# Layer norms of a three-block transformer kernel: residual added ahead, down tiles in turn, gain inside the product, high part direct, low parts awaited apart

## The chip, the cores and the metric

One core of one Trainium2 chip runs the whole program. The metric is device time in microseconds for one execution, start to end. Five engines matter: TensorE (PE, matmul; PEld is its weight load), VectorE (DVE), ScalarE (ACT), GpSimd (POOL) and SyncE (SP), which here issues all the loads. Each engine runs its own instruction stream in order and waits on semaphores.

## The reference

The reference is a stack of three blocks on x of 512 positions by 1024 features, in float32.

```
block 1 (fox):   h = forgetting-gate attention(x);  x = LN(a*x + h); f = conv_ffn(x); x = LN(a*x + f)
block 2 (diff):  h = differential attention(x);     x = LN(a*x + h); f = conv_ffn(x); x = LN(a*x + f)
block 3 (ssd):   h = attention branch + state space branch of rms_norm(x)
                 x = x + rms_norm(h);  x = x + rms_norm(swiglu_ffn(rms_norm(x)))
LN(y) = (y - mean(y)) * rsqrt(var(y) + 1e-5) * g + b       a = 4 ** 0.25, mean over the 1024 features
rms_norm(y) = y * rsqrt(mean(y*y) + 1e-6) * g
```

## The kernel before

**Layout.** Activations are feature major: 8 blocks of 128 features (partitions) by 512 positions. A block `j` of the tensor `XH` is `blk(XH, j)`. Every linear product keeps float32 accuracy by splitting each operand in two parts, a high part rounded to the matmul's type (`XH`, `HI`) and a low part, the rest (`XL`, `LO`). A product of one 128x128 weight block with one 128x512 block of x is three matmuls: HI with XH, HI with XL, LO with XH.

**Order of the work.** A planner, `agenda()`, writes one list of steps; the five engine programs walk it and each picks out its own part of each step. Weights come in units of up to 8 k-blocks by 256 columns. `take` starts a unit, and during its matmul steps (`step_of`, each followed by `tick`) the parts of the next unit are split: ACT writes HI (L1530), DVE (L1899) or POOL (L2382) writes LO. The units named `bqk`, `bv`, `aqk`, `av` have all their LO parts made by POOL, the others alternate. `tick` also advances a side stream (`beside`, the attention of the block). PSUM banks go round in `lin["banks"]`; in the first units of block 3 only banks 0 and 1 are in the ring. `XH` and `YH` are the same memory, and so are `XL` and `YL`.

**The norms.** There are eight, named a0, f0, a1, f1 (layer norms after attention and feed-forward of blocks 1 and 2), c0, m, p, f (RMS norms of block 3). For each tile of the last product before a layer norm, `residual` does, on DVE, two steps `YL = a*XL + PS` (L1928) and `YH = a*XH + YL` (L1932), and `accumulate` puts an `acc` step: ACT squares YH (L1548), POOL adds the square to `A2` (L2402) and, for layer norms, YH to `A1` (L2404). Tiles 0 to 6 are added so; tile 7's YH and its square go to the sums directly. `statistics` is then the following chain:

- `stat0`: PE adds the columns of A2, of A1, of YH block 7 and of the last square with matmuls of one column (`mm(PS[6]...MEAN[:, 0:1])`, 8 records for each). ACT meanwhile loads the table of the square root (L1551).
- `stat1`: DVE copies both sums (L1937), squares the mean (L1939), subtracts (L1942); PE spreads the mean over PS5 (8 records). `stat2`: ACT takes the root (L1557), DVE the reciprocal (L1945). `stat3`: PE spreads it over PS6 (8 records).
- `ln` for each of 8 blocks: DVE subtracts (L1953, `t = PS5 - YH`), DVE multiplies (L1956, `t = t*PS6`), ACT applies gain and bias (L1566, the gain negated). `lnx`: ACT copies t to XH (L1570), POOL writes XL = t - XH (L2382). For f1 the result goes to XR instead and feeds the sums of c0.

The first unit after a norm (`up0`, `up1`, `up2`, `bqk` 0, `ck` 0) is walked k-block by k-block (`together=True`), each matmul step waiting for XL of its k-block. The RMS norms c0 and p make their blocks with one DVE product (L1963), ACT's copy (L1574) and POOL's low part. For m and f, ACT first copies the tile out of PSUM (`cye`, L1578) and squares the copy.

A down projection (`ffn_down`, `lin_long`) makes two tiles at once over 22 k-blocks in three units, matmul step by matmul step in alternation, so that both tiles end together.

Of the kernel before, what the change touches and what calls it, by code (L numbers as in the profile page):

```python
# [110 lines left out]
def const_arrays():  # L111
# [52 lines left out]
    "stat0": (("ssum", 1),),  # L164
    "stat1": (("smu", 1), ("svar", 1)),
    "stat2": (("ssd", 1), ("srs", 1)),
    "stat3": (("spr", 1),),
    "ln": (("lt", 1), ("la", 1)),
# [65 lines left out]
class Agenda:  # L234


    def __init__(self):
        self.steps, self.tiles, self.order, self.bank_of, self.free_of = [], [], [], {}, {}
        self.unit_end, self.count = {}, {}
# [15 lines left out]
def raised(step, tiles):  # L255
# [3 lines left out]
    if k in ("mm", "mt"):  # L259
        return (("lin", 1),) if step[2] in tiles[step[1]].incs else ()  # L260
# [8 lines left out]
    if k == "acc":  # L269
        _, n, j, mean = step  # L270
        adds = (1 if j == 0 else 2 if j < 7 else 0) if mean else (1 if 0 < j < 7 else 0)
        return (("sq", 1),) + ((("ac", adds),) if adds else ())
# [23 lines left out]
def unit_sequence():  # L296
# [9 lines left out]
    out += [("ck", 0), ("cq", 0), ("cq", 1), ("cv", 0)] + [("cx", i) for i in range(6)] + [("cz", i) for i in range(4)]  # L306
# [7 lines left out]
def agenda():  # L314
# [116 lines left out]

    def lin_fm(key, src, widths=(128, 128), together=False, before=None, evac=None):
# [3 lines left out]
        for j, w in enumerate(widths):  # L436
            tiles.append(Tile(made, sum(widths[:j]), w, banks[j], src))
        pairs = [(j, kk) for kk in range(len(made)) for j in range(len(widths))] if together else \
                [(j, kk) for j in range(len(widths)) for kk in range(len(made))]
        for j, kk in pairs:  # L440
            if before is not None:
                before(kk)
            step_of("mm", t0 + j, kk)
            tick()
            if evac is not None and kk == len(made) - 1:
# [14 lines left out]
    def lin_long(keys, src):  # L460
        banks = [pick(), pick()]
        t0 = len(tiles)
# [3 lines left out]
        kk = 0  # L466
        for key in keys:
            take(key)
            for k in range(places[key][1]):
                for j in range(2):  # L470
                    step_of("mm", t0 + j, kk)
                    tick()
                kk += 1
        return [t0, t0 + 1]
# [17 lines left out]
    def statistics(n, mean):  # L492
        at_bank(put("stat0", n, mean), 6)
        if mean:
            at_bank(put("stat1", n), 5)
# [3 lines left out]
        if mean:  # L499
            freed[5] = ("spr", ("stat3", n, mean))  # L500

    def layer_norm(n, final=None):
        statistics(n, True)
        for j in range(8):
            s = put("ln", n, j)
            freed[5] = freed[6] = ("lt", s)
            if final is None:
                x_step[j] = put("lnx", n, j)
            else:
                accumulate(final, j, False)  # L510

# [129 lines left out]
    def ffn_down(lay, evac):  # L641
        for i in range(4):
            for j, t in enumerate(lin_long([("dn" + lay, i, p) for p in range(3)], "H" + lay)):
                evac(2 * i + j, t)
# [1943 lines left out]
```

## Time and profile before

| what | value |
|---|---|
| median of 3 runs | 2434.15 us (2431.7 to 2441.45) |
| profiled execution, its own time | 2443.44 us |
| its span, first to last instruction | 2441.6 us |
| PE busy | 2254.6 us, 92% |
| DVE, ACT, POOL busy | 1096.0, 1001.4, 974.8 us (45%, 41%, 40%) |
| granted TensorE clock, mean | 0.946 of 2.4 GHz |

The page gives one profiled execution. A clock of 1.00 in a stretch is 2.4 GHz, 0.50 is 1.2 GHz. In a timeline row the first number is the start, the second the duration, and the bracket says how long the engine sat idle before it and which engine's instruction ended the wait. Float32 matmuls of the sums show as two records for each instruction.

### The profile page before, as it was taken

How to read it: one execution, taken by the hardware profiler on the slowest of the kernel's cores; microseconds unless marked ns; L12 is line 12 of the kernel's file. 1: busy time of each engine (PE TensorE's matmuls, PEld its weight loads, DVE VectorE, ACT ScalarE, POOL GpSimd, SP SyncE). 2: the span in 40 equal slices, each digit the busy share in tenths (PEclk: the TensorE clock that was granted, in tenths of full speed). 3: DMA queues.
4: the chain of work that ended last, by engine and by line, in shares of the span. 5: the costliest groups of instructions: out<-in, count | busy, mean ns of one | idle time of the engine just before them, and what ended most of it. 6: DMA issues, size and time to landing. Idle time of an engine off the chain costs nothing.

```text
span 2441.6 us, 28073 instructions
## 1 busy us (share of the span) xinstructions
PE 2254.6 (92%) x10880; PEld 1841.6 (75%) x10880; DVE 1096.0 (45%) x1774; ACT 1001.4 (41%) x2015; POOL 974.8 (40%) x760
## 2 busy tenths in 40 slices
PE   7999999999979887999999789996899997999997
PEld 6778778888867776788888666664687885888886
DVE  3545555553345764555443333546545234232222
ACT  5665454443254553444442244443344234232222
POOL 3554644333455641644334351103423345232232
PEclk9999999999989998999999887997999997999998
DMA  4111222222212220222322111110012221222221
GB/s 152 51 65 58 70 87 91 100 101 95 97 61 75 77 83 18 70 101 90 104 97 95 59 46 35 35 35 18 18 44 95 86 104 52 104 87 104 97 95 50
DMA packets 29844, 183.07 MB, mean 75 GB/s; under 512 B 3984, under 2 KB 4112, under 8 KB 11920
## 3 DMA queue, kind: packets, MB, share of 16 engines
q1 hardware_dynamic: 29712, 181.27, 21.5%
q8 instruction: 87, 1.43, 0.2%
q14 instruction: 45, 0.37, 0.0%
HBM read 174.97 MB, written 2.10 MB: 73 GB/s over the span
## 4 chain that ended last, share of the span: by engine, by line
PE 84%; DVE 5%; ACT 4%; POOL 4%; issue 2%; DMA 1%; SPq 0%; POOLq 0%; ACTq 0%; DVEq 0%
PE PS L1239 82%; PE PS L1332 1%; POOL LO L2382 1%; POOL XL L2382 1%; PE PS L1442 1%; DVE bQS L1899 1%; DVE cCVT L2266 0%; DVE aQS L1899 0%; DMA RAW<-wall 0%; POOL A_p L2402 0%; POOL bROT L2430 0%; ACT bP L1739 0%; POOL A_c L2402 0%; PE PS L1380 0%; POOL bTQ L2435 0%
## 5 line engine op out<-in xcount | busy, mean ns | idle before, releaser
L2382 POOL TENSOR_TENSOR LO<-RAW,HI 128x512 fp32r<-128x512 f32 (+1 forms) x382 | 542.3, 1436 | 686.9 <-ACT HI L1530 686.9
L1239 PE MATMUL PS<-XH,HI 128*128 128x512 f32 (+1 forms) x1584 | 645.1, 407 | 40.7 <-POOL XL L2382 20.5
L1239 PE MATMUL PS<-XH,LO 128*128 128x512 f32 (+1 forms) x1584 | 628.1, 397 | 0.0
L1239 PE MATMUL PS<-XL,HI 128*128 128x512 f32 (+1 forms) x1584 | 628.1, 397 | 0.0
L1899 DVE TENSOR_TENSOR LO<-RAW,HI 128x512 fp32r<-128x512 f32 (+3 forms) x286 | 313.5, 1102 | 290.9 <-ACT HI L1530 290.7
L1530 ACT ACTIVATE HI<-RAW 128x512 fp32r<-128x512 f32 (+3 forms) x668 | 365.1, 608 | 170.6 <-PE PS L1239 167.2
L1239 PEld LDWEIGHTS PS<-XH,HI 128*128 128x128 f32 (+1 forms) x1584 | 303.7, 192 | 132.5 <-issue 57.3
L1239 PEld LDWEIGHTS PS<-XH,LO 128*128 128x128 f32 (+1 forms) x1584 | 302.9, 191 | 66.6 <-issue 1.1
L1239 PEld LDWEIGHTS PS<-XL,HI 128*128 128x128 f32 (+1 forms) x1584 | 304.2, 192 | 58.4 <-issue 1.0
L1239 PE MATMUL PS<-HH,HI 128*128 128x512 f32 x528 | 205.4, 389 | 0.0
L1239 PE MATMUL PS<-HL,HI 128*128 128x512 f32 x528 | 205.4, 389 | 0.0
L1239 PE MATMUL PS<-HH,LO 128*128 128x512 f32 x528 | 205.4, 389 | 0.0
L2418 POOL TENSOR_TENSOR UT<-UT 128x512 f32<-128x512 f32 x44 | 56.4, 1282 | 204.8 <-ACT UT L1591 204.8
L1239 PE MATMUL PS<-HI,XH 128*128 128x256 f32 (+1 forms) x416 | 125.7, 302 | 11.3 <-DVE aVL L1899 2.8
L1589 ACT ACTIVATE UT<-PS,SM 128x512 f32<-128x512 f32 x88 | 67.7, 772 | 131.4 <-PE PS L1239 131.4
L1239 PE MATMUL PS<-HI,XL 128*128 128x256 f32 (+1 forms) x416 | 119.4, 287 | 0.0
L1239 PE MATMUL PS<-LO,XH 128*128 128x256 f32 (+1 forms) x416 | 119.4, 287 | 0.0
L1239 PEld LDWEIGHTS PS<-HH,HI 128*128 128x128 f32 x528 | 99.1, 188 | 20.7
L1239 PEld LDWEIGHTS PS<-HH,LO 128*128 128x128 f32 x528 | 99.1, 188 | 20.6
L1239 PEld LDWEIGHTS PS<-HL,HI 128*128 128x128 f32 x528 | 99.1, 188 | 20.4
L1987 DVE SCALAR_TENSOR_TENSOR UT<-PS,SM,UT 128x511 f32<-128x511 f32 x88 | 65.4, 743 | 91.8 <-ACT UT L1589 91.8
L2424 POOL TENSOR_SCALAR aP<-aP,aRC 128x128 f32<-128x128 f32 (+1 forms) x64 | 69.3, 1084 | 92.0 <-DVE aRC L2068 91.8
(380 smaller groups left out, 3352.3 us busy)
## 6 DMA issues: line engine op xcount, KB each, us to landing
RAW<-wall SPq DMA_DIRECT2D x138, 1024.0 KB, 4.8
RAW<-wall SPq DMA_DIRECT2D x24, 896.0 KB, 4.4
bROT<-bTQ SPq DMA_DIRECT2D x64, 64.0 KB, 2.0
RAW<-wall SPq DMA_DIRECT2D x5, 512.0 KB, 3.2
XF<-xT SPq DMA_DIRECT2D x4, 512.0 KB, 6.0
outT<-XR SPq DMA_DIRECT2D x8, 256.0 KB, 2.0
FP<-cfp SPq DMA_DIRECT2D x1, 1024.0 KB, 6.8
MKF<-cmask SPq DMA_DIRECT2D x1, 704.0 KB, 11.4
```

Of the source, the lines that this page charges most:

```text
L1239: return e.matmul(out, a, b, start=start, stop=stop)
L1332: m = e.transpose(PS[bank][:, 128 * kb:128 * kb + 128], aP[:, 512 * (n % 4) + 128 * kb:512 * (n % 4) + 128 * kb + 128], IDN)
L1442: m = e.transpose(PS[bank][:, 128 * kb:128 * kb + 128], p[:, 128 * kb:128 * kb + 128], IDN)
L1530: act(HI[i % 2][:, c], RAW[i % 2][:, c], ACT.Copy).then_inc(SEM["hi"], 1)
L1589: act(x, PS[ag.tiles[t].bank][:, :], ACT.Identity, bias=col(f"cb{lay}", f), scale=col(f"cw{lay}2", f)).then_inc(SEM["ui"], 1)
L1899: return e.tensor_tensor(out, x, h.bitcast(F32), ALU.subtract)
L1987: e.scalar_tensor_tensor(out=x[:, 1:512], in0=ps[:, 0:511], scalar=col(f"cw{lay}1", f), in1=x[:, 1:512], op0=ALU.mult, op1=ALU.add).then_i ...
L2382: return e.tensor_tensor(out, x, h.bitcast(F32), ALU.subtract)
L2418: e.tensor_tensor(g, g, v, ALU.mult).then_inc(SEM["um"], 1)
L2424: e.tensor_scalar(p, p, aRC[:, n:n + 1], None, ALU.mult).then_inc(SEM["dg"], 1)
```

## The change

- **Residual.** `res` first makes YL = XL + XH (both in SBUF, before it waits for the tile, except for tile 0), then YH = a*YL + PS. After the tile is full one DVE step is left, not two.
- **Down tiles in turn.** In the last two-tile group of a down projection, within its last unit (7 k-blocks), all steps of the first tile go ahead of all of the second.
- **Sums.** DVE adds YH block 7 into A1 (`acc` 7), `statm` sums A1 alone into PS5, `stats` sums the last square; A1 and A2 are awaited apart. The mean is copied and squared while `stats` runs, and `stat1` on PE needs only the mean.
- **Layer norm.** For a0, f0, a1: ACT copies the spread mean from PS5 to `MS` (`lnc`); DVE subtracts for blocks 0 and 1, POOL for blocks 2 to 7 in place in YH (`lnm`); DVE multiplies with the gain inside (t = y * gain * PS6); ACT makes XH = t + b directly; DVE, no longer POOL, makes XL = (t + b) - XH, one block behind. For f1, the subtraction reads PS5 as soon as the mean is there, the gain is in the product, and ACT adds only the bias.
- **Low parts awaited apart.** A new step `m2` takes both tiles of a k-block: four matmuls that read XH, then two that read XL, and for operand X the wait for XL stands only ahead of the last two. All `together` units use it.
- **Block 3.** The units `ck` 0 and `cq` 0 change places, `cq` 0 is now walked together, and the rotary steps of its five blocks run in the order 0, 1, 4, 2, 3.
- **m and f.** ACT squares the tile straight from PSUM, and copies it afterwards.

```diff
     def residual / vector, kind "res":
-                e.wait_ge(*when_(ag.tiles[t].full))
-                e.scalar_tensor_tensor(out=blk(YL, j), in0=blk(XL, j).bitcast(F32), scalar=ALPHA, in1=PS[ag.tiles[t].bank][:, :],
-                                       op0=ALU.mult, op1=ALU.add).then_inc(s_vv, 1)
+                if j == 0:
+                    e.wait_ge(*when_(ag.tiles[t].full))
+                e.tensor_tensor(blk(YL, j), blk(XL, j).bitcast(F32), blk(XH, j).bitcast(F32), ALU.add).then_inc(s_vv, 1)
                 vv += 1
+                if j:
+                    e.wait_ge(*when_(ag.tiles[t].full))
                 e.wait_ge(s_vv, vv)
-                e.scalar_tensor_tensor(out=blk(YH, j), in0=blk(XH, j).bitcast(F32), scalar=ALPHA, in1=blk(YL, j),
+                e.scalar_tensor_tensor(out=blk(YH, j), in0=blk(YL, j), scalar=ALPHA, in1=PS[ag.tiles[t].bank][:, :],
                                        op0=ALU.mult, op1=ALU.add).then_inc(SEM["res"], 1)
...
+            elif kind == "acc" and a[1] == 7 and a[2]:
+                e.tensor_tensor(NORM[n]["A1"][:, :], NORM[n]["A1"][:, :], blk(YH, 7), ALU.add).then_inc(SEM["a7"], 1)
+            elif kind == "statm":
+                e.wait_ge(*when("sma", *step))
+                e.tensor_copy(MU, PS[5][:, 0:4]).then_inc(SEM["smu"], 1)
...
 vector, kind "ln":
+                if n == "f1" or j < 2:
+                    mu = PS[5] if n == "f1" else NORM[n]["MS"]
+                    e.tensor_tensor(t, mu[:, :], y, ALU.subtract).then_inc(s_vv, 1)
...
+                e.scalar_tensor_tensor(out=t, in0=y, scalar=NG[GAINS[n][0]][:, j:j + 1], in1=PS[6][:, :],
+                                       op0=ALU.mult, op1=ALU.mult).then_inc(SEM["lt"], 1)
+            elif kind == "lnx":
+                e.scalar_tensor_tensor(out=blk(XL, j), in0=NORM[n][TS[j % 3]][:, :], scalar=col(GAINS[n][1], j),
+                                       in1=blk(XH, j).bitcast(F32), op0=ALU.add, op1=ALU.subtract).then_inc(SEM["xl"], 1)
...
 scalar:
+            elif kind == "lnc":
+                act(NORM[n]["MS"][:, :], PS[5][:, :], ACT.Copy).then_inc(SEM["mus"], 1)
             elif kind == "lnx":
-                act(blk(XH, j), NORM[n][TS[j % 3]][:, :], ACT.Copy).then_inc(SEM["xh"], 1)
+                act(blk(XH, j), NORM[n][TS[j % 3]][:, :], ACT.Identity, bias=col(GAINS[n][1], j)).then_inc(SEM["xh"], 1)
...
 gpsimd:
-            elif kind == "lnx":
-                diff(blk(XL, j), NORM[n][TS[j % 3]][:, :], blk(XH, j)).then_inc(SEM["xl"], 1)
+            elif kind == "lnm":
+                e.tensor_tensor(blk(YH, j), NORM[n]["MS"][:, :], blk(YH, j), ALU.subtract).then_inc(SEM["lm"], 1)
...
 tensor:
+            elif kind == "m2":
+                for T in pair:
+                    mm(PS[T.bank][0:T.w, :], HI[i % 2][:, w], blk(xh, kk), start, False)
+                    mm(PS[T.bank][0:T.w, :], LO[i % 2][:, w], blk(xh, kk), False, False)
+                if first_x is not None and pair[0].src == "X":
+                    e.wait_ge(*when_(first_x))
+                for T in pair:
+                    m = mm(PS[T.bank][0:T.w, :], HI[i % 2][:, w], blk(xl, kk), False, stop)
...
 lin_long:
+            if last and p == len(keys) - 1:
+                pairs = [(j, kk) for j in range(2) for kk in rows]
...
 second:
-        qk_units(("ck", 0), 4, (128,), together=True)
-        qk_units(("cq", 0), 0)
+        qk_units(("cq", 0), 0, together=True)
+        qk_units(("ck", 0), 4, (128,))
```

## Rows read from the trace of the kernel before

**Rows 1.** The page, the chain that ended last, shares of the span by engine.

```profile
PE 84%; DVE 5%; ACT 4%; POOL 4%; issue 2%; DMA 1%; SPq 0%; POOLq 0%; ACTq 0%; DVEq 0%
```

**Rows 2.** Windows: length, busy PE, PEld, DVE, ACT, POOL, clock, DMA share, GB/s.

```profile
325.00:670.00 345.00, 345.00 (x1524) 285.77 (x1523) 159.38 (x188) 134.53 (x231) 142.44 (x102) 1.00 0.29 101
302.33:316.22 13.89, 8.96 (x52) 8.50 (x51) 6.11 (x13) 5.32 (x9) 1.91 (x3) 0.74 0.16 65
676.54:696.97 20.43, 11.25 (x53) 10.80 (x51) 7.16 (x15) 5.95 (x10) 4.25 (x4) 0.61 0.04 18
1006.34:1018.35 12.01, 7.08 (x52) 6.62 (x51) 6.11 (x13) 3.92 (x8) 1.91 (x3) 0.74 0.18 75
1379.15:1416.76 37.61, 17.17 (x79) 16.34 (x77) 15.84 (x29) 16.08 (x26) 11.98 (x10) 0.61 0.00 1
2419.43:2441.60 22.17, 6.16 (x28) 5.64 (x26) 9.82 (x13) 3.83 (x7) 6.32 (x5) 0.55 0.25 95
```

**Rows 3.** Timeline of norm a0, last matmul before to first after.

```profile
302.33 0.39 PE L1239 MATMUL PS<-aOH,LO 128*128 128x512 f32 x1
...
302.75 0.69 DVE L1928 SCALAR_TENSOR_TENSOR YL<-XL,PS 128x512 f32<-128x512 f32 x1 [3.48 <-PE PS L1239]
...
303.48 0.69 DVE L1932 SCALAR_TENSOR_TENSOR YH<-XH,YL 128x512 f32<-128x512 f32 x1
304.20 0.63 ACT L1548 ACTIVATE SQ_a<-YH 128x512 f32<-128x512 f32 x1 [4.26 <-DVE YH L1932]
...
305.82 1.85 PE L1239 MATMUL PS<-FP,SQ_a 128*128 128x1 f32 x8
...
308.01 3.75 PE L1239 MATMUL PS<-FP,TN 128*128 128x128 f32 x16 [0.35 <-DVE TN L1937]
...
312.53 0.69 DVE L1956 TENSOR_TENSOR T_a<-T_a,PS 128x512 f32<-128x512 f32 x1
...
313.25 0.81 ACT L1566 ACTIVATE T_a<-T_a,SM,TN 128x512 f32<-128x512 f32 x1 [4.66 <-DVE T_a L1956]
...
314.80 2.65 POOL L2382 TENSOR_TENSOR XL<-T_a,XH 128x512 fp32r<-128x512 f32 x2 [11.89 <-ACT XH L1570]
...
316.22 0.76 PE L1239 MATMUL PS<-XH,HI 128*128 128x512 f32 x1 [4.46 <-POOL XL L2382]
```

**Rows 4.** Timeline of norm f0, start of the sums.

```profile
681.42 3.57 PE L1239 MATMUL PS<-FP,A_f 128*128 128x1 f32 x16 [4.37 <-POOL A_f L2404]
```

**Rows 5.** Timeline of norm a1: last sum, and both spreads.

```profile
1009.68 1.03 PE L1239 MATMUL PS<-FP,SQ_a 128*128 128x1 f32 x8
...
1011.06 2.84 PE L1239 MATMUL PS<-FP,TN 128*128 128x128 f32 x16 [0.35 <-DVE TN L1937]
```

**Rows 6.** Timeline of norm p: DVE and POOL side by side.

```profile
2039.96 0.98 DVE L1975 TENSOR_TENSOR XR<-XR,YH 128x512 f32<-128x512 f32 x1
2040.54 1.53 POOL L2402 TENSOR_TENSOR A_p<-A_p,MS_p 128x512 f32<-128x512 f32 x1
```

**Rows 7.** Timeline after the first unit of block 2.

```profile
712.20 0.39 PE L1239 MATMUL PS<-HI,XH 128*128 128x256 f32 x1 [1.98 <-ACT bTQ L1707]
```

**Rows 8.** Timeline of the first unit of block 3.

```profile
1416.76 0.77 PE L1239 MATMUL PS<-XH,HI 128*128 128x512 f32 x1 [2.95 <-POOL XL L2382]
...
1417.32 0.63 PE L1239 MATMUL PS<-XL,HI 128*128 128x512 f32 x1
...
1417.75 0.63 PE L1239 MATMUL PS<-XH,LO 128*128 128x512 f32 x1
...
1426.81 0.60 ACT L1767 ACTIVATE cP<-PS 128x512 f32<-128x512 f32 x1 [1.70 <-PE PS L1239]
...
1427.44 0.69 DVE L2197 COPY cQ<-PS 128x512 f32<-128x512 f32 x1 [1.13 <-ACT cP L1767]
```

**Rows 9.** Timeline of norms m and f: table load and root.

```profile
2031.00 1.28 ACT L1551 ACT_TABLE_LOAD   x1
...
2425.44 0.26 ACT L1560 ACTIVATE TN<-PS,NEGC 128x4 f32<-128x4 f32 x1 [2.35 <-PE PS L1239]
```

More of the change, by code:

```diff
@@ L271, in raised @@
         adds = (1 if j == 0 else 2 if j < 7 else 0) if mean else (1 if 0 < j < 7 else 0)
[L272 removed]
+        return (("sq", 1),) + ((("ac", adds),) if adds else ()) + ((("a7", 1),) if mean and j == 7 else ())
     if k == "cxs":
@@ L430, in step_of, with step_of_two @@
             T.full = ("lin", s)
+    def step_of_two(t, kk):
+        s = put("m2", t, kk)
+        i, k = tiles[t].parts[kk]
+        w, x = (i, k // 2), (tiles[t].src, kk) + x_ready(tiles[t].src, kk)
+        for T in tiles[t:t + 2]:
+            if kk == 0:
+                T.free = freed[T.bank]
+            if w not in seen:
+                T.first_w[kk] = (low_part(*w), ("lo",) + w)
+            if x not in seen:
+                T.first_x[kk] = x_ready(T.src, kk)
+            if kk == len(T.parts) - 1:
+                T.incs.add(kk)
+                ag.unit_end[i] = T.full = ("lin", s)
+        seen.update((w, x))
     def lin_fm(key, src, widths=(128, 128), together=False, before=None, evac=None):
@@ L437, in lin_fm @@
             tiles.append(Tile(made, sum(widths[:j]), w, banks[j], src))
[L438 to L445, printed above, removed]
+        if together:
+            for kk in range(len(made)):
+                if before is not None:
+                    before(kk)
+                step_of_two(t0, kk)
+                tick()
+                tick()
+            if evac is not None:
+                evac(0, t0)
+                evac(1, t0 + 1)
+            return [t0, t0 + 1]
+        for j in range(len(widths)):
+            for kk in range(len(made)):
+                step_of("mm", t0 + j, kk)
+                tick()
+            if evac is not None:
                 evac(j, t0 + j)
@@ L465, in lin_long @@
             tiles.append(Tile(made, 128 * j, 128, banks[j], src))
-        kk = 0
-        for key in keys:
+        for p, key in enumerate(keys):
             take(key)
[L469 to L474, printed above, removed]
+            rows = range(row, row + places[key][1])
+            row += len(rows)
+            if last and p == len(keys) - 1:
+                pairs = [(j, kk) for j in range(2) for kk in rows]
+            else:
+                pairs = [(j, kk) for kk in rows for j in range(2)]
+            for j, kk in pairs:
+                step_of("mm", t0 + j, kk)
+                tick()
+                if kk == len(made) - 1:
+                    evac(j, t0 + j)
     def lin_tm(key, src, evac):
@@ L494, in statistics @@
         if mean:
-            at_bank(put("stat1", n), 5)
+            at_bank(put("statm", n), 5)
+        put("stats", n, mean)
+        if mean:
+            put("stat1", n)
         put("stat2", n, mean)
@@ L499, in statistics @@
         if mean:
-            freed[5] = ("spr", ("stat3", n, mean))
+            freed[5] = ("smub", ("stat1", n))
     def layer_norm(n, final=None):
         statistics(n, True)
[L504 to L509, printed above, removed]
-                accumulate(final, j, False)
+        if final is not None:
+            for j in range(8):
+                s = put("ln", n, j)
+                freed[5] = freed[6] = ("lt", s)
+                accumulate(final, j, False)
+            return
+        put("lnc", n)
+        for j in range(2, 8):
+            put("lnm", n, j)
+        for j in range(9):
+            if j < 8:
+                s = put("ln", n, j)
+                freed[5] = freed[6] = ("lt", s)
+            if j:
+                x_step[j - 1] = put("lnx", n, j - 1)
     def rms_apply(n):
```

139 lines of the change are left out of this document (89 added, 50 removed).

## The prediction

> **What bounds the kernel now.** I read the chain that ended last first: TensorE carries 84% of it [rows 1]. Then the windows. A feed-forward stretch has 1524 matmuls in 345.00 us at clock 1.00: one every 0.226 us without a hole, while DVE, ACT and POOL are busy under half of it [rows 2]. Nothing that the change does there can move the time. What it can move are the holes at the norms: from the last matmul before a norm to the first behind it 13.89 us at a0, 20.43 at f0, 12.01 at a1, 37.61 at f1 with c0, and 22.17 from the last matmul to the end at f [rows 2]. In them the engines work one after another, which the timeline shows link by link, and PE falls to the 1.2 GHz level (clock 0.74, 0.61, 0.74, 0.61). So I sum the shortening of each hole, and then ask what the next stretch gives back.
>
> **The chain of a layer norm, before.** At a0, from the last matmul's start D = 302.33 [rows 3]: tile full at D+0.42; two DVE steps (0.73 start to start, then 0.69) and the square; the sums end at S = 307.6, D+5.3; the spreads start 0.35 behind the sums' copy at 308.01 and take 3.75 for 16 records at the low clock; then subtraction 0.73, product 0.72, gain 0.85, copy and XL to 316.22. At a1, where the clock held longer, eight sum records took 1.03 rather than 1.85, and 16 spreads 2.84 rather than 3.75 [rows 5].
>
> **The same chain, after.** D to YH: 0.42 + 0.69 + 0.03 = 1.14 (the addition XL + XH runs before the tile is full, in DVE's idle 3.48 us [rows 3]; without that cover it would cost 0.73). DVE's addition into A1: no row, but same form as a 0.69 row, 0.74 with the semaphore, so 1.88. The sum of A1: 8 records, 0.95 at high clock or 1.85 at low; the sum of squares behind it the same. S = D+3.8 to D+5.6. Sums of A2 need only POOL's earlier add, so they fall ahead of this. The spread of the mean now follows on PE at once, since the mean was copied under the last sum; with the second spread S+3.75 at low clock. At high clock ACT's copy of the mean (0.60, as a PSUM copy) and DVE's subtraction lie beyond the second spread: 0.95 + 0.65 + 0.75 = S+2.4. Then DVE product 0.75, ACT 0.81, waits 0.15: 1.7, where before it was 4.45 (316.22 less 311.77, end of the spreads) [rows 3], because PE's first four matmuls want only XH. Together D+7.9 (all high) to D+11.05 (all low). Both a0 and a1 changed level on the way; I take 9.6.
>
> - a0: 13.89 - 9.6 = 4.3. a1: 12.01 - 9.6 = 2.4.
> - f0: 20.43 - 9.6 = 10.8. This is the largest, since here both down tiles ended together, and POOL's two adds of tile 6 released the sums only at 681.42, D+4.88 [rows 4], after which 32 records ran low. With tile 6 ready 7 x 3 x 0.226 = 4.7 us before tile 7, its square (0.63) and two POOL adds (1.3 to 1.7 each) are over by about D+0.
>
> Sum for the three 17.5; all high 22, all low 13.
>
> **f1 and c0.** The sums gain as at f0: S from D+11.9 to D+4.6, 7.3; the copy before the spread 0.3, the subtraction under the second spread 0.7: 8.3. The eight blocks behind keep ACT's pace of 0.81 and 0.63 each, so no more there. c0's own statistics do not change. The first unit in block 3 starts when XH of block 0 is there, one POOL step earlier (2.65 for two, 1.33, and the wait: 1.4 [rows 3]). Before, a 24-matmul unit came first and starved on XL: 1416.76 to 1426.61; then 48 more, 10.85, to 1437.5. After: start at 1415.35, some 11 matmuls 0.43 apart (the low spacing of 1417.32 and 1417.75 [rows 8]), 61 at 0.226: 1433.9. Gain 3.6. Given back: both tiles of the wide unit now end together, and the next unit wants bank 0, one of only two. It waits 0.42 for the tile, then square 0.60, then copy 0.69 [rows 8]: 1.8 less the normal 0.2, 1.6. Net 2.0 (bounds 0 and 3.6).
>
> **m, p, f.** At m the square comes 0.6 earlier, but the copy moves between square and table load (1.28 [rows 9]), which is then ready exactly as before and still sets the root: 0. At p nothing but the first unit's start: 1.4. At f the root stood at 2425.44 [rows 9], behind 16 records that waited for POOL. After: square from 2419.87, copy, table load, root possible at 2422.5; the sums (8 records from 2420.6) are over by then. Gain 2.9.
>
> **What the next stretch gives back.** Behind a0, f0, a1 DVE carries for each block the product and XL, ACT one step, POOL (for six blocks) one subtraction. The product reads PSUM, about 0.66 apart; XL reads two SBUF operands, like the row where DVE took 0.98 beside POOL's 1.53, against 0.69 and 1.27 alone [rows 6]. So 1.65 a block while POOL runs (until about 7.5 us behind the second spread), 1.31 after: last XH about 10.1 us after the first matmul, last XL 10.8. PE needs the last block 11.7 us after its start (11 slow matmuls, then 31 fast), so it is not starved; the split of the next unit just fits (13.05 needed, 12.4 there). In block 2 it does not: before the second unit ACT makes a table load, four copies of constants and four HI parts, and only then empties the tile, for which PE already waited 1.98 us [rows 7]. ACT's last XH falls at 10.1 behind the first matmul, before 8.5; DVE's small steps for that table come after its last XL. I put 2.0 on the existing wait (bounds 0.7, the tile finished later within `m2`, and 4). The side stream of block 3 is two steps later in its drain: 0.5 (0 to 2).
>
> A page speaks against this division of work. The Trainium skill, "SBUF — State Buffer", section "Who interferes with whom", says that a DVE instruction with two SBUF inputs and a GpSimd instruction that reads SBUF exclude each other for the whole instruction. By that rule a block would cost 0.66 + 0.69 + 1.27 less overlap with PSUM reads, some 0.3 more than my 1.65 for six blocks. The row of norm p (0.98, not 0.69 + 1.27) shows less than a full block, so the sum goes by the row; the full block is the first rival.
>
> **Sum.** 17.5 + 8.3 + 2.0 + 0 + 1.4 + 2.9 - 2.0 - 0.5 = 29.6 us. Against the profiled execution, 2443.44 us, it is 2413.8; that execution lies 9 us above the median, all of whose difference I take as common to both kernels, so 2434.15 - 29.6 = 2404.5, 1.2% less.
>
> **Rivals.**
> - *DVE and POOL exclude each other, and the new DVE pace starves PE.* For: DVE now makes XL beside POOL's subtractions. With 1.96 a block for six blocks XH 7 and XL 7 come about 2 us later, PE waits 0.3 in the first unit and 1.5 at the next split behind a0 and a1, and 2 more in block 2: 5.6 in all. With 2.4 a block three firsts starve by 4 each: 12. Against: the row. Time 2410 to 2417.
> - *The clock does not fall in the shorter holes.* For: a hole of 8 us is shorter than any of now. Then the first matmuls behind also run fast, 2 us each for three holes beside the 4.5 above: 2398 to 2393. Against: at a1 it had fallen well before 12 us.
> - *Absorbed.* The head starts of f0 and f1 are lost to streams that follow them, block 2's POOL LO parts and block 3's convolution drain, if those ran at their own pace. It would take 18 of the 30: 2422 to 2434. Against: both streams are driven by x, and all their inputs move with it.
> - *Slower: the reordered start of block 3.* Its attention stream of some 100 steps waits for the key block, now third. If every step came 0.45 us late against PE, as the two-bank ring and the changed rotary order could make it, 45 us would be lost and the time would be 2449. It decides from 0.3 us a step (30 us lost). Against: the scores start when all five blocks are rotated, in either order within two ticks.
>
> **Numbers.** The sum as worked, 2398 to 2410: 0.60. First rival 0.16; clock 0.10; absorbed 0.09; slower 0.05. Half a percent, 12 us, is about what a measurement can tell from none. Faster is the first three and a third of absorbed: 0.89; same 0.06; slower by over 12 us 0.05. Likeliest 2404.5; its own range 2398 to 2410; for 8 in 10 I reach from 2395 to 2417.
>
> **What would show it.** In the profile after: f0's hole about 10 us and a0's and a1's 9 to 10; the table load first in the chain at f; PE's first matmul behind a norm waiting for ACT's XH, not POOL's XL; two 1.3 to 1.7 waits for DVE's copy at the start of block 3; a longer wait for ACT at the second unit of block 2. I am wrong if PE shows waits on XL within the first units, if DVE's XL rows last over 1.2 us, or if block 3 from its first unit to its convolution drain is longer than before.

## The result and the profile after

The changed kernel takes 2425.2 us (median of 13 runs, 2410.25 to 2430.35); the kernel before, in the same comparison, 2439.49 us (13 runs, 2431.7 to 2446.72). The ratio is 0.9939, with an interval of 0.9921 to 0.9956. So it is faster, by 14.3 us, and not by the 29.6 us of the forecast; 2425.2 lies above the range, which ended at 2417. One of the 13 runs took 2410.25 us, the others 2421.17 and more. Of the 20.7 us of error in the time, 5.3 us is the base: the three runs shown first gave 2434.15 for the kernel before, thirteen gave 2439.49. The other 15.3 us is a gain of half the size.

The profiled execution of the changed kernel has a span of 2423.4 us, 18.2 less than that of before, with a granted clock of 0.949. The page, the chain that ended last, shares by engine (compare [rows 1]):

```profile
PE 85%; DVE 6%; ACT 4%; issue 2%; POOL 2%; DMA 1%; SPq 0%; another core or an unknown queue 0%; POOLq 0%; ACTq 0%; DVEq 0%
```

Windows of the holes at a0, f0, a1, f1 with c0, and from the last matmul to the end at f (columns as in [rows 2]):

```profile
302.22:310.67 8.45, 6.09 (x45) 5.72 (x43) 4.39 (x9) 3.73 (x6) 3.14 (x3) 0.79 0.18 76
673.14:684.65 11.51, 8.35 (x45) 8.10 (x43) 5.16 (x10) 3.73 (x6) 4.65 (x4) 0.70 0.27 91
997.55:1008.07 10.52, 8.17 (x45) 7.81 (x43) 4.38 (x9) 2.34 (x5) 3.06 (x3) 0.68 0.15 64
1370.07:1395.89 25.82, 11.50 (x70) 10.78 (x69) 14.65 (x26) 14.33 (x24) 8.89 (x8) 0.67 0.11 41
2405.21:2423.40 18.19, 3.45 (x28) 3.13 (x26) 9.82 (x13) 2.72 (x5) 5.05 (x4) 0.62 0.31 115
```

Against [rows 2] the holes shrank from 13.89, 20.43, 12.01, 37.61 and 22.17 to 8.45, 11.51, 10.52, 25.82 and 18.19. That is 5.4 + 8.9 + 1.5 + 11.8 + 4.0 = 31.6 us, where the forecast had 4.3 + 10.8 + 2.4 + 9.7 + 2.9 = 30.1. (The 9.7 is its 8.3 for f1 and the 1.4 by which the first unit of block 3 was to start sooner, which the hole up to that unit contains.) So the holes shrank by about what was forecast. Single holes differ between executions: in a second one of each kernel those at a0, f0 and a1 went from 14.00, 20.43 and 14.04 to 8.55, 11.43 and 7.94. The timeline of a0 shows how (compare [rows 3]):

```profile
302.22 0.39 PE L1284 MATMUL PS<-aOH,LO 128*128 128x512 f32 x1
...
302.65 0.69 DVE L2015 SCALAR_TENSOR_TENSOR YH<-YL,PS 128x512 f32<-128x512 f32 x1 [2.51 <-PE PS L1284]
...
303.37 0.69 DVE L2021 TENSOR_TENSOR A_a<-A_a,YH 128x512 f32<-128x512 f32 x1
...
304.21 1.02 PE L1284 MATMUL PS<-FP,A_a 128*128 128x1 f32 x8 [0.59 <-DVE A_a L2021]
...
305.10 1.03 PE L1284 MATMUL PS<-FP,SQ_a 128*128 128x1 f32 x8
...
305.99 2.91 PE L1284 MATMUL PS<-FP,TN 128*128 128x128 f32 x16
...
309.02 0.75 DVE L2053 SCALAR_TENSOR_TENSOR T_a<-T_a,TN,PS 128x512 f32<-128x512 f32 x1 [0.54 <-PE PS L1284]
309.69 1.70 DVE L2045 TENSOR_TENSOR T_a<-MS_a,YH 128x512 f32<-128x512 f32 x1
309.80 0.72 ACT L1651 ACTIVATE XH<-T_a,SM 128x512 fp32r<-128x512 f32 x1 [2.04 <-DVE T_a L2053]
...
310.67 0.76 PE L1284 MATMUL PS<-XH,HI 128*128 128x512 f32 x1 [1.77 <-ACT XH L1651]
...
312.08 1.00 DVE L2058 SCALAR_TENSOR_TENSOR XL<-T_a,SM,XH 128x512 fp32r<-128x512 f32 x1
...
313.13 1.22 PE L1284 MATMUL PS<-XL,HI 128*128 128x512 f32 x2 [0.42 <-DVE XL L2058]
```

From the tile full at 302.65 one DVE step is left, the spreads stand on PE right behind the sums, and PE's first matmul waits for ACT's XH. Two things are dearer than forecast: DVE's second subtraction, 1.70 us, and a wait of 0.42 for the first XL. The same wait is 0.36 at f0 and 1.37 at a1. At f0 it was DVE's addition into A1 that came dearer, 1.50 us beside POOL's low parts, and PE waited 1.40 for it:

```profile
672.73 2.51 POOL L2486 TENSOR_TENSOR LO<-RAW,HI 128x512 fp32r<-128x512 f32 x2
...
674.28 1.50 DVE L2021 TENSOR_TENSOR A_f<-A_f,YH 128x512 f32<-128x512 f32 x1
...
675.93 1.83 PE L1284 MATMUL PS<-FP,A_f 128*128 128x1 f32 x8 [1.40 <-DVE A_f L2021]
```

What the units behind the holes give back is seen in windows from the first matmul to the 49th, of up0, of the first unit of block 2 and of up1:

```profile
310.67:325.20 14.53, 14.11 (x48) 10.92 (x49) 14.16 (x18) 7.17 (x11) 8.80 (x7) 0.77 0.00 0
684.65:702.74 18.09, 12.93 (x48) 9.89 (x48) 12.82 (x22) 11.67 (x19) 9.71 (x7) 0.91 0.00 1
1008.07:1022.13 14.06, 12.69 (x48) 10.07 (x49) 13.69 (x18) 7.15 (x11) 8.33 (x6) 0.88 0.01 2
```

The same three of before:

```profile
316.22:328.61 12.39, 12.39 (x49) 10.13 (x49) 9.73 (x12) 10.70 (x17) 11.50 (x9) 0.88 0.01 1
...
696.97:712.20 15.23, 13.25 (x48) 10.44 (x48) 8.79 (x17) 14.76 (x24) 11.00 (x9) 0.85 0.00 1
1018.35:1031.22 12.87, 12.87 (x48) 10.43 (x49) 9.74 (x12) 10.71 (x17) 11.96 (x9) 0.85 0.01 2
```

At a0 the unit is 2.1 us longer, and most of that is PE busy at a lower clock (0.77 against 0.88; busy 14.11 us against 12.39). At a1 it is 1.2 us longer at a higher clock (0.88 against 0.85): there it is the wait of 1.37 for the first XL. In block 2 it is 2.9 us, where PE now waits 4.80 for ACT's copy and waited 1.98 before [rows 7]:

```profile
702.74 0.39 PE L1284 MATMUL PS<-HI,XH 128*128 128x256 f32 x1 [4.80 <-ACT bTQ L1788]
```

The clock behind a0's hole is no property of the change. In a second execution of the kernel before, behind a hole of 14.00 us, the same unit ran at 0.78 and took 13.88 us:

```profile
317.78:331.66 13.88, 13.88 (x49) 11.15 (x49) 9.73 (x12) 10.68 (x17) 12.39 (x9) 0.78 0.00 0
```

The large part is elsewhere. I cut block 3 at ACT's fourth copy of a value tile (`cV`) and at DVE's last convolution step. Windows from c0's first XH to the one, and from there to the other, of after:

```profile
1395.10:1446.90 51.80, 49.05 (x313) 41.40 (x314) 22.33 (x36) 27.03 (x53) 27.79 (x23) 0.96 0.20 69
1446.90:1670.70 223.80, 192.85 (x848) 134.32 (x847) 96.81 (x177) 88.91 (x179) 30.67 (x22) 0.83 0.08 30
```

And of before:

```profile
1414.60:1470.60 56.00, 51.35 (x321) 42.25 (x322) 22.05 (x37) 28.29 (x53) 30.40 (x24) 0.94 0.20 69
1470.60:1682.10 211.50, 182.82 (x840) 125.04 (x839) 102.65 (x175) 88.54 (x178) 30.20 (x20) 0.87 0.09 30
```

The first stretch, the reordered start, became 4.2 us shorter. The second, whose code the change does not touch, became 12.3 us longer, at a clock of 0.83 in place of 0.87. The account of the two profiled executions closes: at the first cut the changed kernel leads by 1470.6 - 1446.9 = 23.7 us, the stretch takes back 12.3, what follows, with norms p and f, brings 6.8: 18.2.

### The profile page after: what moved, and what is told of

Read it like the earlier page. It is cut to its first block, busy times and chain, and to the rows that moved or that the text cites. A ratio compares the mean times of both kernels' runs of the same rounds, so it can differ in the third digit from the quotient of the medians.

```text
span 2423.4 us, 28048 instructions
## 1 busy us (share of the span) xinstructions
PE 2244.8 (93%) x10837; PEld 1837.0 (76%) x10848; DVE 1104.6 (46%) x1784; ACT 984.6 (41%) x1994; POOL 971.7 (40%) x754
## 4 chain that ended last, share of the span: by engine, by line
PE 85%; DVE 6%; ACT 4%; issue 2%; POOL 2%; DMA 1%; SPq 0%; another core or an unknown queue 0%; POOLq 0%; ACTq 0%; DVEq 0%
PE PS L1284 83%; PE PS L1409 1%; PE PS L1519 1%; POOL LO L2486 1%; DVE bQS L1980 1%; POOL A_p L2506 0%; DMA RAW<-wall 0%; DVE aQS L1980 0%; DVE cCVT L2370 0%; POOL A_c L2506 0%; DVE XL L2058 0%; PE PS L1457 0%; POOL bTQ L2539 0%; ACT bP L1820 0%; POOL bROT L2534 0%
## 5 line engine op out<-in xcount | busy, mean ns | idle before, releaser
L2486 POOL TENSOR_TENSOR LO<-RAW,HI 128x512 fp32r<-128x512 f32 (+2 forms) x382 | 538.2, 1425 | 718.9 <-ACT HI L1607 718.9
L1284 PE MATMUL PS<-XL,HI 128*128 128x512 f32 (+1 forms) x1584 | 621.7, 397 | 2.2 <-DVE XL L2058 2.2
L1980 DVE TENSOR_TENSOR LO<-RAW,HI 128x512 fp32r<-128x512 f32 (+2 forms) x286 | 303.2, 1064 | 292.1 <-ACT HI L1607 291.9
L1284 PE MATMUL PS<-HH,HI 128*128 128x512 f32 x528 | 205.4, 389 | 0.0
L1284 PE MATMUL PS<-HL,HI 128*128 128x512 f32 x528 | 205.4, 389 | 0.0
L1284 PE MATMUL PS<-HH,LO 128*128 128x512 f32 x528 | 205.4, 389 | 0.0
L1284 PE MATMUL PS<-HI,XH 128*128 128x256 f32 (+1 forms) x416 | 125.9, 303 | 12.3 <-ACT bTQ L1788 4.8
## 6 DMA issues: line engine op xcount, KB each, us to landing
MKF<-cmask SPq DMA_DIRECT2D x1, 704.0 KB, 10.8
```

The source lines that it names most:

```text
L1284: return e.matmul(out, a, b, start=start, stop=stop)
L1980: return e.tensor_tensor(out, x, h.bitcast(F32), ALU.subtract)
L2486: return e.tensor_tensor(out, x, h.bitcast(F32), ALU.subtract)
```

## The experiments

Each edit is against the changed kernel or the one before, as said. "The old start" is block 3's start of before (ck 0, then cq 0, rotary order 4, 0, 1, 2, 3), "the new start" that of the change.

**The two kernels again.**

> The changed kernel, unaltered, a second time. The first pair of profiles has the changed kernel 22.5 us ahead of the old one at the start of unit cx 0 of block 3, but 11.4 ahead when the convolution stream of block 3 ends: 11 us are given back between. Theory A (the new order at the start of block 3 causes it): the same loss in this profile, lead falling by 9 to 13 us between these points, and the time about 0.6% under before. Theory B (the granted TensorE clock in that stage differs from run to run, no cause in the change): the clock there, 0.85 to 0.88 in the first profile, comes out differently, and the lead with it by 4 us or more; the timed ratio then lies anywhere from 0.988 to 0.994.

> The kernel before, unaltered, for a second profile. Theory A: block 3 from cx 0 to the end of the convolution stream takes 226 us again (1456.3 to 1682.1), within 2 us. Theory B: it differs by 4 us or more, with the clock.

The changed kernel: 2425.02 us (2420.46 to 2435.11), ratio 0.9946 [0.9925, 0.9966]. The kernel before, in one more profiled execution: 2435.71 us. The result stands. In the second execution of the changed kernel the stretch again took 223.6 us at 0.83. But in the second execution of the kernel before it ran at 0.95:

```profile
1447.20:1670.80 223.60, 192.73 (x848) 134.34 (x847) 96.79 (x176) 88.90 (x179) 30.69 (x22) 0.83 0.08 30
...
1478.00:1674.30 196.30, 167.65 (x840) 116.53 (x839) 102.63 (x175) 88.25 (x178) 30.18 (x20) 0.95 0.09 33
```

That is 15.2 us shorter than in the first execution, with the same instructions, and PE's busy time is shorter by the same 15.2 (182.82 and 167.65), so PE's idle time is the same. It is the clock that decides the length. It also means that the 12.3 us above is one draw: between the second two executions the stretch takes back 27.3.

**swap_back: the changed kernel with the old start.**

```diff
-    out += [("cq", 0), ("ck", 0), ("cq", 1), ...
+    out += [("ck", 0), ("cq", 0), ("cq", 1), ...
...
-        qk_units(("cq", 0), 0, together=True)
         qk_units(("ck", 0), 4, (128,))
+        qk_units(("cq", 0), 0)
...
-            for n in (0, 1, 4, 2, 3):
+            for n in (4, 0, 1, 2, 3):
```

> The changed kernel with the start of block 3 as before: unit ck 0 first and alone, then cq 0 tile by tile, rotary order 4, 0, 1, 2, 3. Theory A: faster than the changed kernel by 5 to 9 us (the 11 us come back, less the 2 to 4 that the new start gains), ratio to before about 0.991. Theory B: slower than the changed kernel by 2 to 5 us, which the head start at cq 0 is worth, ratio 0.995 to 0.996.

> The same kernel as the one with the whole change but the old start of block 3, a second time, to see whether its 2409.7 us stands. All theories in which the new start costs something by itself: 2407 to 2413 us, 0.987 to 0.990 of the kernel before. If the loss is only a matter of the state that the clock happened to be in, it can as well come out near the whole change, 2420 to 2427 us.

2409.68 us (2406.29 to 2412.11), ratio 0.9875 [0.9856, 0.9893]; the same kernel again 2412.96 (2404.97 to 2416.93), 0.9891 [0.9866, 0.9915]. Over both, 11 runs, the median is 2411.6: 13 us better than the whole change. No kernel here was clearly better. Its two windows, and the second one in the execution profiled for the repetition:

```profile
1396.80:1452.80 56.00, 51.50 (x321) 42.50 (x322) 22.04 (x38) 28.30 (x53) 30.38 (x24) 0.93 0.20 69
1452.80:1649.10 196.30, 167.69 (x841) 116.60 (x839) 102.66 (x175) 88.21 (x178) 30.22 (x20) 0.95 0.09 33
...
1446.80:1652.20 205.40, 176.68 (x840) 122.61 (x838) 102.23 (x176) 88.54 (x178) 30.16 (x20) 0.90 0.09 31
```

The start is 4.2 us longer than with the change, the stretch behind 27.5 shorter, in the repetition 18.4. (Some 2.3 us of it is where the cut falls: with the new start PE is idle 31.0 us of the stretch and not 28.6, and what follows the stretch is 2.8 us shorter.)

**swap_only: the kernel before with the new start alone.** Here cq 0 is walked k-block by k-block with the steps of its two tiles in turn, since the step `m2` doesn't exist in this kernel.

> The kernel before with nothing but the new start of block 3: cq 0 first and walked together, ck 0 second, rotary order 0, 1, 4, 2, 3 (tile steps in alternation, since the step for two tiles isn't there). Theory A, the new start costs by itself, wherever the stretch lies: it shortens the first two units by 2 to 4 us and loses 13 to 17 in the stretch behind, by a lower granted clock: 2448 to 2455 us, 1.004 to 1.007. Rival B, the loss arises only together with the new norms: -4 to +2 us, 0.998 to 1.001. The forecast's own term: -2.0 us, 0.999.

2445.4 us (2440.2 to 2448.48, 12 runs), ratio 1.0024 [1.0008, 1.004]: 6 us slower. The new start shortens the first window by 3.3 us and yet costs, without the new norms too. Theory A has the sign; its 9 us or more were not reached.

```profile
1420.30:1473.00 52.70, 49.30 (x313) 41.57 (x314) 22.36 (x36) 27.10 (x52) 27.74 (x23) 0.94 0.19 68
1473.00:1686.90 213.90, 183.15 (x848) 127.51 (x847) 97.55 (x176) 88.75 (x179) 30.87 (x22) 0.87 0.09 31
```

**q_in_turn: the whole change, cq 0 tile after tile.**

```diff
-        qk_units(("cq", 0), 0, together=True)
+        qk_units(("cq", 0), 0)
```

> The whole change, but cq 0 is walked tile after tile, not both tiles together; it still comes ahead of ck 0. Theory O, the order of the units and of the rotary steps costs: stays at 2422 to 2428 us, 0.993 to 0.996. Theory G, both tiles ending together on a ring of two banks costs: near the kernel with the old start, 2409 to 2414 us, 0.988 to 0.990, though its first unit starves on XL like the one of before (2 us).

2417.07 us (2413.29 to 2419.75), 0.9913 [0.9889, 0.9937]. Between the two theories: 8 of the 13 us come back by the medians, but the interval overlaps that of the whole change.

**rotary_only: the old start, but the new rotary order.**

```diff
-            for n in (4, 0, 1, 2, 3):
+            for n in (0, 1, 4, 2, 3):
```

> The kernel with the new norms and the old unit order (ck 0, then cq 0), but with the new order of the rotary steps (0, 1, 4, 2, 3). Theory R, the rotary order costs: 2420 to 2426 us, 0.992 to 0.995. If the loss lies in the units' order or walk: 2408 to 2414 us, 0.987 to 0.990.

2421.57 us (2420.08 to 2437.93), 0.9943 [0.9912, 0.9973]. Ten of the 13 us are lost with the old unit order too, as theory R had it. But q_in_turn keeps the new rotary order and loses less. So neither the order of the units nor the rotary order alone accounts for the loss.

```profile
1395.30:1448.80 53.50, 49.17 (x297) 40.92 (x298) 21.90 (x34) 25.36 (x49) 28.67 (x22) 0.93 0.22 72
1448.80:1664.10 215.30, 191.03 (x864) 131.80 (x863) 98.36 (x178) 91.75 (x183) 25.85 (x18) 0.85 0.08 30
```

**Work added.** `start_delayed` puts 19 further matmuls, whose product is overwritten, ahead of unit cq 1 of the whole change; `half_delay` puts 9 there; `back_delayed` puts 19 there with the old start.

```diff
+                    if kk == 0 and T.c == 0 and ag.order[i] == ("cq", 1):
+                        for _ in range(19):
+                            mm(o, hi[:, w], blk(xh, kk))
                     mm(o, hi[:, w], blk(xh, kk), start, False)
```

> The whole change with 19 further matmuls of 128x512 (4.3 us at the high clock) on PE ahead of the third unit of block 3, cq 1; their product is overwritten. So the stretch behind begins as late after c0 as with the old start. Theory T, the loss comes from the 4 us by which the matmuls lie earlier against the streams beside them and against the clock's history: it runs like the kernel with the old start, 2409 to 2417 us, 0.988 to 0.991, faster than the whole change although work was added. Theory O, order and walk of the units cost by themselves: 2425 + 4 less what the extra matmuls hide, 2425 to 2430 us, 0.994 to 0.997.

> The whole change with 9 further matmuls (2.0 us) ahead of cq 1 in place of 19. If the loss goes smoothly with the head start, it lies half way: 2417 to 2422 us, 0.991 to 0.994. If it is a matter of how single holes fall, anything from 2408 to 2428.

> The kernel with the new norms and the old start, and the same 19 further matmuls (4.3 us) ahead of cq 1. If the place in time decides as start_delayed let one think, with the old place the good one, this shift leaves it: 2416 to 2428 us, 0.991 to 0.995, by lower clock. If a later stretch is never worse: 2411.6 + 4.3, so 2414 to 2418, 0.989 to 0.991.

| start of block 3 | added | median, us | ratio |
|---|---|---|---|
| new | 0 | 2425.02 | 0.9946 [0.9925, 0.9966] |
| new | 2.0 us | 2413.05 (2410.36 to 2419.92) | 0.9891 [0.9868, 0.9914] |
| new | 4.3 us | 2414.21 (2413.01 to 2420.8) | 0.9905 [0.9884, 0.9925] |
| old | 0 | 2411.6 (2404.97 to 2416.93) | 0.9875 [0.9856, 0.9893] and 0.9891 [0.9866, 0.9915] |
| old | 4.3 us | 2418.18 (2402.74 to 2425.66) | 0.9901 [0.9874, 0.9928] |

`half_delay` settles most: 2 us of useless work make the changed kernel 12 us faster, with the units' order and walk untouched, and the intervals of the two ratios don't meet. Nine matmuls regain as much as nineteen, so it does not go smoothly with the shift. The old start, shifted by the same 4.3 us, loses 6.6 us, at the edge where the two expectations meet, so this run doesn't decide between them. Its profiled execution is no typical one: it took 2402.74 us, the five others 2418.07 to 2425.66, so the clock of 0.94 in its stretch says nothing of the median. That the whole change stands in a bad place is shown; that the old start's isn't the only good one is shown by half_delay and start_delayed. Windows of half_delay:

```profile
1392.40:1446.20 53.80, 51.05 (x322) 43.10 (x323) 22.38 (x36) 27.05 (x53) 27.83 (x23) 0.96 0.18 67
1446.20:1657.00 210.80, 179.99 (x848) 125.58 (x846) 97.52 (x177) 88.78 (x179) 30.80 (x22) 0.89 0.09 32
```

of start_delayed:

```profile
1450.80:1659.20 208.40, 177.50 (x848) 124.36 (x846) 97.50 (x176) 88.81 (x179) 30.81 (x22) 0.90 0.09 32
```

and of back_delayed:

```profile
1448.30:1645.50 197.20, 168.49 (x840) 117.32 (x839) 102.64 (x176) 88.25 (x178) 30.20 (x20) 0.94 0.09 33
```

Nine windows of this stretch are shown now. With the level of a clock c held for 2 x (1 - c) of the length at 1.2 GHz, and 0.47 us lost in each such microsecond (matmuls 0.43 apart [rows 8] in place of 0.226 [rows 2]), an estimate of what is left is nearly one number:

| kernel | length | clock | at 1.2 GHz | length - 0.47 x that |
|---|---|---|---|---|
| before_again | 196.3 | 0.95 | 19.6 | 187 |
| swap_back | 196.3 | 0.95 | 19.6 | 187 |
| back_delayed | 197.2 | 0.94 | 23.7 | 186 |
| start_delayed | 208.4 | 0.90 | 41.7 | 189 |
| half_delay | 210.8 | 0.89 | 46.4 | 189 |
| before | 211.5 | 0.87 | 55.0 | 186 |
| swap_only | 213.9 | 0.87 | 55.6 | 188 |
| rotary_only | 215.3 | 0.85 | 64.6 | 185 |
| after | 223.8 | 0.83 | 76.1 | 188 |

Lengths run from 196 to 224 us, and the estimate stays within 2 us either way: the differences are clock. The cut is at a step of ACT, so the windows don't hold quite the same matmuls (840, 848, and 864 in rotary_only). A check that needs no estimate is the length less PE's busy time: 28.6 to 31.0 us in the eight others, 24.3 in rotary_only. In those eight PE stood idle nearly as long in the fast stretches as in the slow ones; in the slow ones the matmuls took longer.

**The attention stream alone.** `swap_early` is the whole change with that stream's drain two ticks (steps of the planner) earlier, `back_late` the old start with it two later, `back_early` the old start with it two earlier. The edit of swap_early:

```diff
             for _ in prep():
-                for _ in range(SLOW):
+                for _ in range(0 if summed[0] else SLOW):
                     yield
```

> The changed kernel with its new start of block 3 kept, but the attention stream two planner ticks earlier, so that it stands against the units cx as in the kernel before. Theory P (the loss comes from where the stream's steps fall against the turns at the ends of the cx units, through PE's idle time there and the clock): the stretch from the last step of cv to the last convolution step falls from 223.7 us to 196 to 212, clock-low time in it from 77 us to under 60, the time is 2395 to 2408 and beats the variant with the old start (2409.7). Theory O (the order of the units itself, or both tiles ending together, is what costs): no better than 2418.

> The changed kernel with the old start of block 3 (2409.7 us), and the attention stream two planner ticks later, as the new start puts it. Theory P: the loss is back without the new start: 2422 to 2432 us, stretch about 224 us, clock-low about 77 us in it, and the first turn's wait for ACT 1.7 us, not 0.7. Theory O: 2408 to 2412.

> The kernel with the new norms and the old start, with the attention stream of block 3 two ticks earlier in its drain. With the new start this gave 8.4 us back. If an earlier stream is good whatever the start: 2402 to 2408 us, 0.985 to 0.988. If it only made up for the new start: 2409 to 2414 us, 0.988 to 0.990. If any shift moves the clock's pattern about without a sign: between 2409 and 2422 us.

2416.7 us (2413.21 to 2418.79), 0.9911 [0.9887, 0.9934]; 2410.72 (2409.75 to 2413.47), 0.9889 [0.9866, 0.9911]; 2415.75 (2413.01 to 2417.88), 0.9907 [0.9886, 0.9929]. By the medians, earlier helps the new start by 8 us and costs the old start 4, both near what the intervals allow for chance; later costs the old start nothing, where theory P wanted 12 us or more. (The stretch of swap_early, 207.8 us at 0.89, is as theory P had it; its time isn't.) So the theory that the stream's lag itself is the price falls.

PE's longest waits don't tell the cases apart either. In the timeline of after, PE's waits of over 1 us from 29 to 66 us into the stretch:

```profile
1478.03 0.80 PE L1284 MATMUL PS<-XH,HI 128*128 128x512 f32 x1 [2.27 <-ACT FP L1903]
...
1510.06 0.66 PE L1536 MATMUL PS<-FP,cCVT 128*128 128x128 f32 x4 [1.68 <-ACT cXS L1922]
...
1511.89 0.76 PE L1284 MATMUL PS<-XH,HI 128*128 128x512 f32 x1 [1.18 <-ACT FP L1903]
```

In swap_back, over the same part:

```profile
1482.36 0.50 PE L1284 MATMUL PS<-XH,HI 128*128 128x512 f32 x1 [1.18 <-ACT FP L1903]
...
1512.19 0.50 PE L1284 MATMUL PS<-XH,HI 128*128 128x512 f32 x1 [1.18 <-ACT FP L1903]
```

That looked like a cause, but back_late has the waits of 2.27 and 1.68 too, and is as fast as swap_back.

**down_only: the kernel before with the last down tiles in turn alone. norms_only: the change without those and without the new start.**

> The kernel before with only the last down tiles in turn (f0, f1 and f). At f0 and f1 the sums no longer wait for POOL's two adds: 4.4 us each by the wait's row, and some sums move to the high clock, 1 to 2 us; at f 2 us. By my sum 11 to 14 us less, ratio 0.9945. Rival: the split of the next unit's weights, now behind tile 6's square on ACT and behind its adds on POOL, delays the adds and gives 3 us of it back, ratio 0.996.

> The whole change without the new start of block 3 and without the last down tiles in turn (old alternation), so the new norm chains alone. If gains add: the down tiles in turn alone measured 19 us (0.9918), the whole change without the new start 30 (0.9875), so the norm chains 11: 2427 to 2431 us, 0.994 to 0.997. By the sum of the forecast, 17.5 + 8.3 + 1.4 + 2.9 less what tile 6's head start gives at f0, f1 (some 4.7 each): 18 to 21 less 2.5 given back, 2421 to 2425 us, 0.992 to 0.994.

2420.54 us (2416.77 to 2429.6), 0.9918 [0.99, 0.9936], and 2424.26 (2423.17 to 2427.76), 0.9946 [0.9927, 0.9965]. The hole at f0 in down_only:

```profile
676.16:688.74 12.58, 7.78 (x53) 7.41 (x51) 6.41 (x13) 5.33 (x9) 4.59 (x5) 0.82 0.24 83
```

One edit of a few lines in `lin_long` takes 7.9 of the 8.9 us that f0 gained, since POOL's two adds of tile 6 are over when tile 7 ends. Alone it is worth 19 to 20 us, where 11 to 14 were expected; what brings the rest wasn't looked for. The norm chains alone bring 13 to 15, a little under what the forecast's terms give for them (15.5 to 18.5). The two sum to 32 to 35 us, both together (swap_back) measured 26 to 30; intervals of 4 us either way don't tell these apart.

**sub_psum: swap_back, with DVE's two subtractions reading the mean from PSUM.**

```diff
-                    mu = PS[5] if n == "f1" else NORM[n]["MS"]
+                    mu = PS[5]
```

> The changed kernel with the old start of block 3, and DVE's two subtractions of each layer norm read the mean from PSUM (after ACT's copy, as before), so that they have one SBUF operand. Theory of the port (DVE with two SBUF operands waits for POOL): the second subtraction falls from 1.70 to 0.7 us, the first XL comes 1.0 us earlier at a0, f0, a1, and the time is 2 to 3 us under 2409.7. Rival (the second subtraction is long for another reason): nothing changes.

2421.43 us (2411.11 to 2422.71), 0.992 [0.9893, 0.9947]. At a0 the edit does what it should. Timeline of a0, DVE, in sub_psum:

```profile
311.92 0.69 DVE L2045 TENSOR_TENSOR T_a<-PS,YH 128x512 f32<-128x512 f32 x1 [1.08 <-ACT MS_a L1647]
...
313.77 0.69 DVE L2045 TENSOR_TENSOR T_a<-PS,YH 128x512 f32<-128x512 f32 x1
```

and in swap_back:

```profile
309.59 0.69 DVE L2045 TENSOR_TENSOR T_a<-MS_a,YH 128x512 f32<-128x512 f32 x1 [1.84 <-ACT MS_a L1647]
...
311.42 1.77 DVE L2045 TENSOR_TENSOR T_a<-MS_a,YH 128x512 f32<-128x512 f32 x1
```

The second subtraction beside POOL's falls from 1.77 to 0.69. In this execution of swap_back it was long at a0 only (0.72 at f0, 0.97 at a1). The whole is 10 us slower than swap_back by the medians, where 2 to 3 us less was expected. The cause is open: two of its six runs took 2411.11 and 2412.70 us, like swap_back, and four 2421.04 to 2422.71, and the profiled one is 2411.11. The slow four show the lower clocks (0.949 to 0.951 against 0.955 and 0.953), but no trace shows where.

**wait_joint: swap_back, with the wait for XL ahead of all six matmuls of a k-block.**

```diff
-                    e.wait_ge(*when("xh", *first_x[1]))
+                    e.wait_ge(*when_(first_x))
```

> The changed kernel with the old start of block 3, but the first unit after a norm waits for XL of a k-block ahead of all six matmuls of it. By my sum the head start of PE is lost: 2.4 us at a0, f0 and a1 each and 1.4 at p. Since PE then waits for XL 0 anyway (0.4 to 1.4 us in the changed kernel) and starts slow, I expect half of it, 3 to 6 us more than 2409.7. Rival: the first units are bound by DVE's pace, and nothing is lost.

2422.73 us (2419.75 to 2429.79), 0.9938 [0.9916, 0.996]: 11.1 us slower than swap_back, where 3 to 6 were expected. PE now waits for the first XL at each norm, at a0:

```profile
314.57 0.77 PE L1284 MATMUL PS<-XH,HI 128*128 128x512 f32 x1 [4.37 <-DVE XL L2058]
```

The wait is 4.37 us at f0 and a1 too, and the three holes are 12.45, 12.11 and 13.17 us, where the two profiled executions of swap_back have 9.93, 11.55, 7.95 and 8.60, 9.20, 8.11. Part of that comes back in the first units, which no longer wait inside. From the last matmul of each of these norms' products to the second unit behind, the three add up to 79.2 us, against 76.9 and 72.0: so 2 to 7 us go with the wait, and the expected 3 to 6 lie in that. Much of the rest is clock in the stretch of block 3, 208.2 us at 0.89 where swap_back had 196.3 and 205.4. (The profiled execution took 2429.79 us, the slowest of its eight runs.)

## Why the prediction was half right

- **The chains.** D (the start of the last matmul before the norm) to the first matmul behind was put at 9.6 us; it is 8.45 at a0 and 10.52 at a1, within the two ends worked out (7.9 and 11.05). f0 was put at 9.6 and is 11.51: 0.8 us of that is DVE's addition into A1, 1.50 us where 0.69 was taken, the rest goes with the low clock (eight sum records took 1.83 us there and 1.02 at a0). f1 with c0 gained 11.8 where 9.7 was forecast, f 4.0 where 2.9 was. Right, and slightly small in sum.
- **The first units behind.** Forecast 0 behind a0 and a1 and 2.0 in block 2; in the first pair of profiles it is 2.1 behind a0, 1.2 behind a1 and 2.9 in block 2. The term for block 2 has the right mechanism, the longer wait for ACT, and is a little small. The wait on XL was put at nothing and is 0.36 to 1.37. The clock behind a hole was not thought of: the clock term of the sum counted only records inside the hole. It has no fixed sign. At a0 the unit behind ran at 0.77 where it had 0.88, in block 2 at 0.91 where it had 0.85, at a1 at 0.88 where it had 0.85, and the second execution of the kernel before had 0.78 at a0.
- **DVE beside POOL.** With two SBUF operands beside POOL, one DVE step at each norm took some 1 us more than its 0.69: the second subtraction at a0 (1.70) and a1 (1.77), the addition into A1 at f0 (1.50, the second subtraction there 0.75). XL took 0.99 to 1.13 in place of 0.74. At a0 the XL steps started 1.70 us apart beside POOL and 1.32 after, where the forecast had 1.65 and 1.31 and the first rival 1.96. So the pace was right, and the rival's full block did not come on six blocks; the part of its price that came is in the holes above. The Trainium skill, "SBUF — State Buffer", section "Who interferes with whom", has the two exclude each other for the whole instruction; the traces agree as far as the three long steps go (1.70, 1.77, 1.50) and show less than a full block for the XL steps (0.99 to 1.13), and sub_psum, where one operand is in PSUM, shows none (0.69).
- **The start of block 3, the step that failed.** "Net 2.0 (bounds 0 and 3.6)" is right in sign and too small: the first window shortened by 4.2 us (1.4 of it is the hole's, counted above). But the sum ended there, with "0.5 (0 to 2)" for everything behind. Up to c0's first XH its terms give 17.5 + 8.3 - 2.0 = 23.8 us, and the changed kernel led by 19.5 there in the first pair of profiles and by 26.3 in the second. From there to the end the forecast gains another 5.8 us; the changed kernel loses 1.3 of its lead in the first pair and 16.0 in the second. The stretch behind gave back 12.3 us between the first two profiles and 27.3 between the second two, and the new start costs 13 us in the whole change (2425.0 against 2411.6) and 6 in the kernel before. The forecast without this part, 29.6 - 2.0 + 0.5 = 28.1 us, is about what swap_back measured: 26 to 30 us. Two of the signs that the prediction gave for being wrong came: block 3 is longer from its first unit to its convolution drain (275.6 us for 267.5), and PE waits on XL within the first units.
- **The rivals.** The one on the other side named the right place and the wrong mechanism: moving the attention stream by itself costs nothing or little, and it is the same work at a lower clock. "Absorbed" has the measured time in its range, 2422 to 2434, and that is luck: it laid the loss to two streams that hold their own pace, but PE was idle as long as before in block 3's stretch, within 2.3 us, and what was lost there is clock. The rival on the clock asked only whether it falls in the holes, not what it does in a stretch at mean 0.83 to 0.95 that no part of the change touches. In one hole it did not fall, a1's in the second execution of the changed kernel (7.94 us at 1.00); it fell behind it, where the unit ran at 0.87. Beside the holes, [rows 2] had only the one stretch at 1.00 in view; block 3's, at 0.87, is not in the forecast, and there lies most of the miss.

What is shown: the new start costs time (swap_back twice, swap_only), the loss is in the granted clock of that stretch (the table of nine, and the equal idle time), and added work regains it (half_delay, start_delayed). What is open: why the place that the whole change gives the stretch is a bad one, and how much a forecast could have known of it, since the kernel before itself ran it at 0.87 and at 0.95. Waits of PE, stream lag, unit order and rotary order were each tried, and none of them alone goes with the clock. Sums by stage rest on one or two executions for each kernel; the medians carry the comparison of kernels.

## What to carry to other kernels

Sum the shortened holes, but before adding them up read the granted clock of every stretch, and give each one that runs below 1.00 and has holes of its own a term of both signs: here 13 us, as large as most parts of the change. Take more than one profile before a stage is priced: here the same stage of the same kernel differed by 15 us. Measure the parts of a large change apart: one cost half of what the others brought, and the one of the fewest lines, the last two tiles in turn, brought the most. If a kernel's time answers to 2 us of useless matmuls with 12 us, an improvement smaller than that has to be judged at more than one placement.

## What was not expected of the hardware

- The same instructions in the same kernel took 211.5 us at a granted clock of 0.87 in one execution and 196.3 us at 0.95 in another.
- Nine added 128x512 matmuls (2.0 us) made a program of 2425 us 12 us faster.
- The clock behind a hole did not follow from the hole's length: 0.88 over 12 us behind one of 13.89 us and 0.78 over 14 us behind one of 14.00 us, in two executions of one kernel. Behind a hole of 7.94 us that itself ran at 1.00 (norm a1, second execution of the changed kernel), the unit ran at 0.87.
- A DVE subtraction of two SBUF operands of 128x512 took 0.69 us alone, and beside GpSimd's anything from 0.72 to 1.77; with the mean in PSUM it took 0.69 there too.
